# Two transformer blocks on one core: where the scratch tiles lie in memory

## The reference

```
# first block
h = rms_norm(x);  q, k, v, xr, yr = split(h @ w_in)
q, k = rms_norm per head, axial rope;  attn = softmax(q k^T) v       # 8 heads, 2 kv heads
xc = depthwise_conv(xr, width 4)
lru = (rg_lru(xc, forward) + rg_lru(xc, backward)) * gelu(yr)        # gated recurrences
x = x + concat(attn, lru) @ w_out
u = depthwise_conv(rms_norm(x) @ w_up, width 3);  gate, val = split(u)
x = x + (gelu(gate) * val) @ w_down;  x = rms_norm(x)                # 3072 hidden channels
# second block
proj = rms_norm(x) @ w_in_2                                          # 11280 columns
o_conv = silu(layer_norm(depthwise_conv(a * sigmoid(g), width 31))) @ w_conv_out
o_gla  = gated linear attention, chunks of 64, 4 heads
o_diff = differential attention, 8 heads, causal by chunks of 64
y = sigmoid(m_conv) * o_conv + sigmoid(m_gla) * o_gla + sigmoid(m_diff) * o_diff
x = x + y @ w_out_2
gate, up = split(rms_norm(x) @ w_ffn_in_2);  x = x + (silu(gate) * up) @ w_ffn_out_2
return rms_norm(x)
```

## Time and profile before

| | |
|---|---|
| median of 3 runs | 4058.28 us |
| the profiled execution's own time | 4057.34 us |
| its span | 4055.6 us |
| TensorE busy | 3624.6 us (89%) |
| VectorE busy | 1742.0 us (43%) |
| ScalarE busy | 1343.0 us (33%) |
| GpSimd busy | 679.3 us (17%) |
| DMA | 174.90 MB, mean 43 GB/s |
| mean granted clock of TensorE | 0.953 |

### The profile page before, as it was taken

The page is one execution under the profiler, slowest core; times in us unless marked ns, Lnnn a source line. Parts: engine busy times, 40 slices in busy tenths (PEclk is TensorE's granted clock), DMA queues, the critical chain, the costliest instruction groups (busy, mean ns, idle before and its releaser), DMA issues.

```text
span 4055.6 us, 44191 instructions
## 1 busy us (share of the span) xinstructions
PE 3624.6 (89%) x17220; PEld 2901.6 (72%) x17220; DVE 1742.0 (43%) x1714; ACT 1343.0 (33%) x1533; POOL 679.3 (17%) x284
## 2 busy tenths in 40 slices
PE   4888846799999996899999999999889979999997
PEld 3776735688888884777787777777656768888885
DVE  5535466432231345422226777777725431111114
ACT  4545452342341323222222333333324233122112
POOL 1000012122222221111111111111111212222221
PEclk8999978899999998999999999999889989999998
DMA  2000001111111110201011100111010201111111
GB/s 91 21 7 16 11 21 73 36 47 47 52 47 47 47 47 26 83 35 37 31 36 47 37 33 35 36 36 36 31 68 31 87 32 49 49 47 47 47 52 68
DMA packets 43130, 174.90 MB, mean 43 GB/s; under 512 B 4784, under 2 KB 4784, under 8 KB 41904
## 3 DMA queue, kind: packets, MB, share of 16 engines
q1 hardware_dynamic: 43056, 173.84, 12.1%
HBM read 161.24 MB, written 12.58 MB: 43 GB/s over the span
## 4 chain that ended last, share of the span: by engine, by line
PE 75%; DVE 14%; ACT 5%; issue 5%; DMA 1%; POOL 0%; DVEq 0%; ACTq 0%; SPq 0%
PE ps L332 62%; DVE conv_acc L1073 3%; PE ps L341 3%; PE ps L348 2%; PE ps L1382 2%; PE ps L1375 1%; PE ps L1524 1%; PE ps L1511 1%; DVE h_lo_part L419 1%; PE ps L1518 1%; DVE small L1113 1%; ACT dprob L728 1%; PE ps L1464 1%; PE ps L1497 0%; DVE lru_e L1264 0%
## 5 line engine op out<-in xcount | busy, mean ns | idle before, releaser
L332 PE MATMUL ps<-h_hi_part,w_hi_part 128*128 128x512 f32 x3504 | 1129.0, 404 | 174.2 <-DVE h_lo_part L419 76.1
L312 POOL TENSOR_TENSOR w_lo_part<-w_raw,w_hi_part 128x1024 fp32r<-128x1024 f32 x272 | 662.4, 2435 | 3318.3 <-ACT w_hi_part L305 3317.5
L332 PE MATMUL ps<-h_lo_part,w_hi_part 128*128 128x512 f32 x3504 | 1097.7, 395 | 0.0
L332 PE MATMUL ps<-h_hi_part,w_lo_part 128*128 128x512 f32 x3504 | 1094.3, 394 | 0.0
L332 PEld LDWEIGHTS ps<-h_hi_part,w_hi_part 128*128 128x128 f32 x3504 | 652.8, 192 | 340.0 <-issue 144.2
L305 ACT ACTIVATE w_hi_part<-w_raw 128x1024 fp32r<-128x1024 f32 x272 | 287.3, 1058 | 1616.2 <-PE ps L332 1526.6
L332 PEld LDWEIGHTS ps<-h_lo_part,w_hi_part 128*128 128x128 f32 x3504 | 669.3, 191 | 144.6
L332 PEld LDWEIGHTS ps<-h_hi_part,w_lo_part 128*128 128x128 f32 x3504 | 667.5, 191 | 143.8
L1073 DVE SCALAR_TENSOR_TENSOR conv_acc<-u_pad,cols,conv_acc 128x1024 f32<-128x1024 f32 x232 | 315.3, 1359 | 19.6 <-DVE conv_acc L1073 2.0
L975 DVE TENSOR_TENSOR residual<-residual,ps 128x1024 f32 x56 | 68.4, 1221 | 395.4 <-PE ps L332 394.7
L332 PE MATMUL ps<-u_hi,w_hi_part 128*128 128x512 f32 x736 | 230.9, 394 | 0.0
(11 more groups left out here) (310 smaller groups left out, 3557.9 us busy)
## 6 DMA issues: line engine op xcount, KB each, us to landing
w_raw<-in_w SPq DMA_DIRECT2D x272, 512.0 KB, 3.4
residual<-in_x SPq DMA_DIRECT2D x4, 1024.0 KB, 10.5
residual<-in_x SPq DMA_DIRECT2D x1, 4096.0 KB, 12.4
residual_spill<-residual SPq DMA_DIRECT2D x1, 4096.0 KB, 12.1
conv_spill<-conv_acc SPq DMA_DIRECT2D x8, 512.0 KB, 2.6
conv_again<-conv_spill SPq DMA_DIRECT2D x1, 4096.0 KB, 12.6
residual_again<-residual_spill SPq DMA_DIRECT2D x1, 4096.0 KB, 12.8
out<-residual SPq DMA_DIRECT2D x8, 512.0 KB, 3.0
```

The lines of the kernel that those rows point to most:

```text
L312: pool.tensor_tensor(WLO[:, slot], WRAW[:, slot], f32(WHI[:, slot]), ALU.subtract).then_inc(w_ready, 1)
L332: last = pe.matmul(PS[:, slot, b * HALF:(b + 1) * HALF], st[:, slot, k, :], mv[:, k, b * HALF:(b + 1) * HALF], start=(k == 0 and n == 0), ...
```

## The change

The scratch region now starts right behind h_lo. The residual, the weight buffers, cols, con and small come after it, in the same order as before. Sizes, names, instructions, waits and transfers are the same; only addresses differ.

```diff
         HI = sb("h_hi_part", [P, KT, S], F32R)
         lo_at = base[0]
         LO = sb("h_lo_part", [P, KT, S], F32R)
+        scr = base[0]
+        base[0] += 20 * TILE + 128
         xy_at = base[0]
         X = sb("residual", [P, KT, S], F32)
         WRAW = sb("w_raw", [P, 2, KT, P], F32)
...
         CON = sb("con", [P, NCONST], F32)
         SMALL = sb("small", [P, 128], F32)
-        scr = base[0]
 
         def scratch(name, shape, dt, tile):
             return sb(name, shape, dt, scr + tile * TILE)
```

## The result

The changed kernel takes 4089.56 us, the median of six runs (4083.78 to 4092.36), against 4057.35 for the kernel before (4054.89 to 4060.16, six runs). The ratio is 1.0079, 95% interval [1.0066, 1.0091]: slower by 0.8%. The forecast was 4043. The result lies in the stated range (4036 to 4122), which had been stretched that far to take in rival 1 (a longer period, h slower). Rival 1 had the direction; its price, +57 us, was nearly twice the measured 32.

The account below looks back on a forecast made before the run. The prediction took TensorE's L332 matmuls, count times step, to bound most of the kernel. From 4057.34 it took 14.7 us for u and 0.3 for xc and f: 4042.3, or 4043 as median; range 4036 to 4122.

Parts of the forecast that it names:

- rival 1: L332 matmuls: period longer than 128 bytes, h slows to u's old step, u gains nothing; +57 us, 4114; chance 0.25.
- The bound and the reading of the step: TensorE's L332 matmuls set most of the span; operand distance modulo 512 sets their step: 0 gives 226.7, 192 gives 233.3 ns.
- its own last test: Weight matmuls in the profile after: the argument itself is wrong if h and u still differ from each other.
- The argument from k and q: Attention matmuls, both operands in scratch, remainder 0: minimum 387 ns like h, so distance counts; it must stay 387.
- The step that failed: Weight matmuls: a 128-byte period makes remainder 384 count as 0, so every matmul steps at 226.7 ns.
- The size of u's gain: Down jobs streaming u: 2208 matmuls, each 6.67 ns faster, save 14.7 us, all on the path.
- The bounds: Weight matmuls' step at remainder 384: one 6.67 ns spacing outward either side, 220.0 and 240.0 ns, as an estimate.
- The zeros: fp32 matmuls, VectorE, ScalarE and DMA: each taken as 0 change; the fp32 matmuls within 2.6 us of nothing.

Follow-up runs that it names:

- e1: The changed kernel with 384 unused bytes between scratch and the residual, making h's and u's remainders against the weights 0; 4040.71 us, 0.9958 of the kernel before.
- e2: The kernel before with everything moved up by 64 bytes together, all distances kept; 4058.89 us, ratio 1.0002.
- e3: The kernel before with 128 bytes ahead of the residual and 192 ahead of scratch, giving the changed kernel's remainders; 4090.21 us, ratio 1.0077.
- e10: The kernel before with 320 bytes ahead of the residual and 320 ahead of scratch, so h and u exchange remainders; 4079.05 us, ratio 1.0056.
- e4: The kernel before with 256 bytes ahead of the residual and 128 ahead of scratch (remainders h 256, u 320); 4042.24 us, ratio 0.9957.
- e13: The kernel before with 64 bytes ahead of scratch and nothing else, giving u remainder 256 (0 modulo 256); 4042.40 us, ratio 0.9961.
- e11: The layout of e1 with 64 bytes added between w_hi and w_lo; 4088.38 us, 1.0066 of the kernel before.
- e5: The kernel before with 448 bytes ahead of the residual and 448 ahead of scratch (remainders h 64, u 128); 4071.72 us, ratio 1.0029.

## Why the prediction was wrong

- **The bound and the reading of the step** held. L332 sets the long stages; the step was 226.7 for h and 233.3 for u; the remainder of the distance between the operands sets it. e1, e2, e3 and e10 together show that, each against another explanation. By its own last test, the prediction is wrong in the argument if h and u still differ from each other, and they don't.
- **The argument from k and q** held: their remainder didn't change and their minimum stayed at 387.
- **The step that failed**, in the prediction's words: "I take the shortest period that fits, 128 bytes: then 384 counts as 0 and every matmul steps at 226.7". Two points, remainders 0 and 192, cannot tell a period of 128 from one of 256 or 512, and the choice of the shortest had nothing else behind it. The period is 256 (e4 has 226.67 at 256), and 384 counts as 128, which gives 232.4 to 232.8. So h lost 5.9 ns a matmul where nothing was forecast, and u gained 0.9 where 6.7 was.
- **The size of u's gain**, 14.7 us, was right for the kernel that has it: e13 lies 14.6 under the runs of before beside it (4057.02).
- **Rival 1's price** was too large: +57 against +32. Its step was 0.8 ns too long: 8,760 matmuls at 5.88 are 51.5 us, 50.5 with its 2% off. It let u gain nothing, where u gave 2.1 back. And it took all else to stay as it was. In the heads, 1,236 of these matmuls should have cost 7.3 us; the stretch got 2.2 shorter, since more of it ran at full clock. The stretch of 108.3 us behind them got 3.6 shorter, where its 144 should have cost 0.8. That leaves 50.5 - 2.1 - 9.5 - 4.4 = 34.5, against 31.9 in the spans. Neither the forecast nor its rivals had a term for the clock of one trace differing from another's: in the heads alone, half clock went from 16 to 57 us over the twelve traces, as an estimate worth some 18 us.
- **The bounds**: a mean step of 220 never occurred; 240 occurs as single steps, not as a mean.
- **The zeros** held: VectorE, ScalarE, DMA and the fp32 matmuls kept their durations.
- **The Trainium skill**, "SBUF — State Buffer", section "Who interferes with whom", has it that TensorE's two read ports are independent and that TensorE never waits on anyone. By that, 64 bytes ahead of scratch change nothing, but e13 took 0.4% less; the measurement decides. The 4057 that follows from the rule holds for e2 alone, which keeps all distances.

**What stays open.** What in the hardware has the period of 256 bytes; that the stream collides with the load of the next weights was only argued, and e11 did not settle it. Why more of the heads runs at full clock in one execution than in another: it doesn't simply follow the step, for with 226.67 on h they have 36 us at half clock in the kernel before, e1 and e13, but 29 in e4 and 43 in e2. Why the stretch behind the heads takes 108.1 to 108.5 us in the kernel before, e1, e2, e4, e5 and e13, and 101.7 to 104.9 in the others. Finer remainders than 32 bytes were not run.

## What to carry to other kernels

Where long rows of 512-column fp32r matmuls bound a kernel, read the start-to-start step, not the duration, and compare it between streams of the same shape; a difference is reason enough to try one padding of scratch. Place the streamed tiles and the weight tiles a multiple of 256 bytes apart, both halves of the weights alike, and check it after each change of layout, since any new small tile in between shifts it. A share of the chain times a longer step is not yet the price: compare the two traces stage by stage, and the granted clock of each stage with them. Here the clock gave back more in the heads than the step cost there.

## What the runs showed of the hardware

- The same fp32r matmul, 128 rows by 512 columns at a granted clock of 1.00, takes on average 226.67 to 234.3 ns from start to start, by the distance between its operands modulo 256: 544 to 562 cycles of the full 2.4 GHz for 512 columns. At a granted clock of 0.50 a pair on h steps at 0.85 us, with no excess over its columns; no other remainder was looked at there.
- At remainders 0 and 192 of the kernel before the step settles on one value; at 128 and in e11 it wanders for as long as the stream lasts, between 228 and 241 at 128 and between 224 and 236 in e11.
- Moving everything by 64 bytes together changes nothing: 1.0002 [0.9993, 1.0012].
- fp32 matmuls of 128 columns, and VectorE's and ScalarE's instructions of 1024 elements, don't show it, at the places compared above and in the earlier trace rows: medians of 273 to 275 ns for the matmuls, means of 1224 to 1227 and 1059 to 1061 for the others.
- With 6.6 us more of the differential heads at half clock and the same steps (e2 against the kernel before), these took 3.1 us longer.
